# Hybrid decoder trunk: a fourth buffer for the gated levels, a new pace of the projections that fill the attention steps, and another order of three parts of a step

## The reference, cut to what matters

```python
z = h @ w_in[l]
(g_q, g_k, g_v, g_lr, g_r, d_q, d_k, d_v, i_q, i_k, i_w, c_u) = jnp.split(z, split_at, axis=-1)
# gated linear attention, 4 heads: decays are exp of differences of a running sum b of log_a
o_gla = gla_chunked(g_q, g_k, g_v, log_a)
# sparse attention, 6 heads: 128 of the causal keys of each query, chosen by an indexer
o_dsa = dsa_attention(dq, dk, d_v, i_q, i_k, i_w * (IDX_HEADS ** -0.5), rel_bias, topk)
# causal depthwise convolution with 31 taps over 256 channels
o_conv = conformer_conv(c_u, conv_w[l], conv_b[l], conv_ln_g[l], conv_ln_b[l])
mix = jnp.concatenate([o_gla, o_dsa, o_conv], axis=-1)
x = x + mix @ w_out[l]
```

## Time and profile before

| | us |
|---|---|
| median of 3 executions | 1520.78 (1519.08 to 1529.86) |
| the profiled execution, its own time | 1523.78 |
| its span in the profile | 1521.9 |
| PE busy, of the span | 1428.2 (94%) |
| DVE busy | 1159.8 (76%) |
| ACT busy | 908.5 (60%) |
| POOL busy | 552.1 (36%) |

### The profile page before, as it was taken

How to read it: one execution, slowest core, us unless ns; L and a number is a source line. 1 busy time by engine, 2 the same in 40 slices (tenths; PEclk the granted TensorE clock), 3 DMA queues, 4 the chain that set the end, 5 groups by cost and what they waited for, 6 DMA issues and landing times.

```text
span 1521.9 us, 20214 instructions
## 1 busy us (share of the span) xinstructions
PE 1428.2 (94%) x6710; PEld 1036.4 (68%) x6710; DVE 1159.8 (76%) x1658; ACT 908.5 (60%) x1346; POOL 552.1 (36%) x240
## 2 busy tenths in 40 slices
PE   7999989999899999999799999999988999999996
PEld 4677455567577888877556864565766778887773
DVE  4697877433479999999758968773334899999997
ACT  5643445743547888788475533448335488887881
POOL 2332242060005666554542413311500066555544
PEclk9999999999989999999999999999989899999999
DMA  6332601312239999999651431105040499999995
GB/s 226 93 91 62 220 1 56 141 56 88 79 123 338 401 399 399 398 399 399 215 193 43 111 100 52 56 1 196 1 165 1 180 350 399 399 399 398 398 401 192
DMA packets 151483, 312.73 MB, mean 205 GB/s; under 512 B 33158, under 2 KB 46380, under 8 KB 151228
## 3 DMA queue, kind: packets, MB, share of 16 engines
q1 hardware_dynamic: 140300, 271.39, 49.3%
q0 software_dynamic: 6624, 24.12, 4.3%
q10 hardware_dynamic: 4496, 16.40, 2.7%
HBM read 287.76 MB, written 29.50 MB: 208 GB/s over the span
## 4 chain that ended last, share of the span: by engine, by line
PE 47%; DVE 24%; DMA 15%; ACT 7%; issue 6%; DVEq 1%; POOL 0%; SPq 0%; POOLq 0%; ACTq 0%
PE ps L708 13%; DMA arena<-in_w_down 12%; DVE rest_w_down L1425 8%; PE ps L726 6%; PE ps L1502 5%; DVE rest_w_up L1425 4%; PE ps L1524 3%; DVE rest_w_gate L1425 2%; ACT head_w_down L1420 2%; PE ps L815 2%; DVE xg_rest L1438 2%; PE ps L1618 2%; PE ps L729 1%; PE ps L788 1%; PE ps L1637 1%
## 5 line engine op out<-in xcount | busy, mean ns | idle before, releaser
L2088 POOL TENSOR_TENSOR rest_w_down<-arena,head_w_down 128x2048 fp32r<-128x2048 f32 x30 | 191.2, 6372 | 191.5 <-ACT head_w_down L1420 191.5
L1425 DVE TENSOR_TENSOR rest_w_down<-arena,head_w_down 128x2048 fp32r<-128x2048 f32 x30 | 152.1, 5069 | 13.3 <-ACT head_w_down L1420 13.2
L1425 DVE TENSOR_TENSOR rest_w_gate<-arena,head_w_gate 128x2048 fp32r<-128x2048 f32 x64 | 145.9, 2280 | 0.1
L1425 DVE TENSOR_TENSOR rest_w_up<-arena,head_w_up 128x2048 fp32r<-128x2048 f32 x64 | 143.5, 2281 | 0.1
L1420 ACT ACTIVATE head_w_down<-arena 128x2048 fp32r<-128x2048 f32 x60 | 115.2, 1926 | 39.3 <-DMA arena<-in_w_down 39.0
L1420 ACT ACTIVATE head_w_gate<-arena 128x2048 fp32r<-128x2048 f32 x60 | 114.8, 1919 | 37.0 <-DMA arena<-in_w_gate 37.0
L1420 ACT ACTIVATE head_w_up<-arena 128x2048 fp32r<-128x2048 f32 x64 | 122.0, 1940 | 10.5 <-DMA arena<-in_w_up 10.5
L1409 PE MATMUL ps<-head_w_gate,xg_head 128*128 128x512 f32 x256 | 104.0, 406 | 3.7 <-DVE xg_rest L1438 2.7
L1399 PE MATMUL ps<-head_w_down,he_head 128*128 128x512 f32 x240 | 99.7, 415 | 6.5 <-DVE rest_w_down L1425 3.8
L726 PE MATMUL ps<-hT,arena 128*128 128x512 f32 x224 | 105.1, 608 | 0.7 <-ACT mixg L936 0.7
L1411 PE MATMUL ps<-head_w_gate,xg_rest 128*128 128x512 f32 x256 | 100.1, 391 | 0.0
(11 more groups left out here) (373 smaller groups left out, 3516.1 us busy)
## 6 DMA issues: line engine op xcount, KB each, us to landing
arena<-in_w_gate SPq DMA_DIRECT2D x64, 1024.0 KB, 10.1
arena<-in_w_up SPq DMA_DIRECT2D x64, 1024.0 KB, 10.7
arena<-in_w_down SPq DMA_DIRECT2D x64, 1024.0 KB, 10.4
arena<-in_w_in SPq DMA_DIRECT2D x10, 1536.0 KB, 6.7
yrows<-yb ACTq DMA_DIRECT2D x30, 512.0 KB, 6.2
arena<-in_w_in SPq DMA_DIRECT2D x4, 2048.0 KB, 8.5
x<-in_x SPq DMA_DIRECT2D x8, 512.0 KB, 13.8
arena<-in_w_in SPq DMA_DIRECT2D x16, 256.0 KB, 4.7
```

The lines of the kernel that those rows point to most:

```text
L1425: nc.vector.tensor_tensor(wl[q][:, c, :], raw[q][:, c, :], wh[q][:, c, :].bitcast(F32), ALU.subtract).then_inc(s_split[q], 1)
L2088: nc.gpsimd.tensor_tensor(wl[2][:, c, :], raw[2][:, c, :], wh[2][:, c, :].bitcast(F32), ALU.subtract)\
```

## The change

- A fourth level buffer: the tile `rs`, which holds the roots of the gated outputs later in the layer, is added to `lev`. Levels use `lev[v % 4]`; the diagonals move to `lev[3]`. `differences(v)` waits from v = 3 on, for the diagonals (v = 3) or for the products of level v-4.
- The planner gets three ranges: steps 0 to 3 for ca and cg, 4 to 8 for gq and gk, 9 to 21 for the rest. gk's last piece falls in step 8 in place of 9. By the planner's arithmetic the pieces of steps 4 to 17 become 6, 7, 6, 6, 7, 7, 6, 6, 6, 5, 6, 4, 5, 4 (before: 6, 6, 6, 5, 6, 7, 6, 7, 6, 5, 6, 5, 4, 5), and the third update falls in step 16 in place of 17.
- `LEV0` loses its "- 1", so it stays at step 8. `FACTORED` becomes 9 (from 10), the step of `states` 17 (from 18).
- `FIRST_TAP` becomes 5 (from 4). The taps of steps 4 to 21 become 0, 6, 6, 6, 5, 2, 0, 1, 1, 1, 2, 3, 3, 3, 6, 6, 5, 6 (before: 2, 6, 6, 6, 4, 4, 2, 0, 0, 0, 1, 2, 3, 6, 3, 6, 5, 6).
- In PE's even steps the values come straight behind the turn, then the first piece of projection, then the logits, then the second piece.

```diff
-            lev = [view(mixg[:, :, :].rearrange("p h s -> p (h s)"), 1024 * i, 2, S) for i in range(2)] + [sq[:, :, :]]
+            lev = [view(mixg[:, :, :].rearrange("p h s -> p (h s)"), 1024 * i, 2, S) for i in range(2)] + [sq[:, :, :], rs[:, :, :]]
...
-            GATED, LAST_FILLED, FIRST_O = 4, 22, 19
+            GATES, GATED, LAST_FILLED, FIRST_O = 4, 9, 22, 19
...
-            first, then = range(GATED), range(GATED, LAST_FILLED)
-            paces = [filler(("ca", "cg"), first) / len(first), filler(("gq", "gk", "gv", "kt", "gr", "upd", "o"), then) / len(then)]
+            phases = ((("ca", "cg"), range(GATES)), (("gq", "gk"), range(GATES, GATED)),
+                      (("gv", "kt", "gr", "upd", "o"), range(GATED, LAST_FILLED)))
+            paces = [filler(names, steps) / len(steps) for names, steps in phases]
...
-                pace += paces[n >= GATED]
+                pace += paces[(n >= GATES) + (n >= GATED)]
...
-            LEV0 = step_of(done("gk") - 1) - 1
+            LEV0 = step_of(done("gk") - 1)
...
-            FIRST_TAP, LAST_TAP, MEAN = step_of(done("cg") - 1) + 1, 21, 22
+            FIRST_TAP, LAST_TAP, MEAN = step_of(done("cg") - 1) + 2, 21, 22
...
                     turn(n)
+                    if n % 2 == 0 and n:
+                        values(n - 2)
+                    for job, c in work_of[n][:1]:
+                        work(job, c)
                     if n % 2 == 0 and n + 2 < NS:
                         logits(n + 2)
                         logits(n + 3)
-                    if n % 2 == 0 and n:
-                        values(n - 2)
-                    for job, c in work_of[n][:2]:
+                    for job, c in work_of[n][1:2]:
                         work(job, c)
...
-                    if v >= 2:
-                        dve.wait_ge(sN["lev_mm"], v - 1)
+                    if v >= len(lev) - 1:
+                        dve.wait_ge(sN["lev_mm"], v - len(lev) + 2)
...
-                        do(nc.gpsimd.tensor_tensor(lev[2], gq, gk, ALU.mult), "lev_k")
+                        do(nc.gpsimd.tensor_tensor(lev[3], gq, gk, ALU.mult), "lev_k")
```

More of the change, by code:

```diff
@@ L771, in diagonals @@
                         for i in range(2):
-                            last = nc.tensor.matmul(ps[2][:, 4 * c + 2 * i:4 * c + 2 * i + 2], lev[2][:, i, P * c:P * c + P], gated,
+                            last = nc.tensor.matmul(ps[2][:, 4 * c + 2 * i:4 * c + 2 * i + 2], lev[3][:, i, P * c:P * c + P], gated,
                                                     start=True, stop=True)
@@ L785, in level_products @@
                             o = ps[LEV_BANK[h % 2]][:, at:at + 64].rearrange("p (n w) -> p n w", w=HALVES[v])
-                            k = lev[v % 3][r, h // 2, P * c:P * c + P]
+                            k = lev[v % len(lev)][r, h // 2, P * c:P * c + P]
                             q = k.rearrange("p (n w) -> p n w", w=2 * HALVES[v])[:, :, HALVES[v]:]
@@ L1073, in level_decays @@
                     act.wait_ge(sN["lev_d"], v + 1)
-                    d = halves(lev[v % 3], half)
+                    d = halves(lev[v % len(lev)], half)
                     nc.scalar.activation(d[:, :, half:], d[:, :, half:], ACT.Exp)
@@ L1231, in differences @@
                         dve.wait_ge(sN["proj_out"], done("cg"))
-                    if v >= 2:
-                        dve.wait_ge(sN["lev_mm"], v - 1)
+                    if v >= len(lev) - 1:
+                        dve.wait_ge(sN["lev_mm"], v - len(lev) + 2)
                     bv = halves(b, half)
-                    do(nc.vector.tensor_tensor(halves(lev[v % 3], half), bv, bv[:, :, half - 1:half].to_broadcast([P, 2 * S // (2 * half), 2 * half]),
+                    do(nc.vector.tensor_tensor(halves(lev[v % len(lev)], half), bv, bv[:, :, half - 1:half].to_broadcast([P, 2 * S // (2 * half), 2 * half]),
                                                ALU.subtract), "lev_d")
@@ L1241, in level_queries @@
                     dve.wait_ge(sN["lev_e"], v + 1)
-                    d = halves(lev[v % 3], half)[:, :, half:]
+                    d = halves(lev[v % len(lev)], half)[:, :, half:]
                     do(nc.vector.tensor_tensor(d, halves(gq, half)[:, :, half:], d, ALU.mult), "lev_q")
@@ L1356, in level_keys @@
                     gp.wait_ge(sN["lev_e"], v + 1)
-                    d = halves(lev[v % 3], half)[:, :, :half]
+                    d = halves(lev[v % len(lev)], half)[:, :, :half]
                     do(nc.gpsimd.tensor_tensor(d, halves(gk, half)[:, :, :half], d, ALU.mult), "lev_k")
```

## The result

| | median of 20 executions, us |
|---|---|
| before | 1523.42 (1518.83 to 1531.75) |
| changed | 1529.12 (1522.61 to 1537.57) |

The ratio is 1.0037, with a 95% interval of 1.0019 to 1.0055: slower by some 5.7 us, where 5.9 us less had been forecast, and 7 us above the upper end of the forecast's range. The profiled execution took 1525.32 us.

What follows compares the result with a forecast made beforehand. PE was taken as the bound, only its idle time and clock losses winnable: 17.4 us gain less 10.0 put back less 1.5 for the clock gave 5.9, so 1514.9 us. Its own range was 1511 to 1519, widened to 1507 to 1522.

Steps and rivals of the forecast that it cites:

- 6.4 us a layer: PE's waits before the turns, level products and turned keys: the most that could be won there in each layer.
- The 1.0 us before the first level products: Step 11, before L788: PE would newly wait about 1.0 us for merge(0), bounds 0 and 2.
- the three slow stretches: Clock drops behind PE's waits at step 11 and the turned keys: 1.55 us each, 4.6 us together to be won.
- the turned keys: PE's wait before L740: of 2.1 us a layer 0.3 would be left, bounds 0 and 2.1.
- the queue behind gk: Steps 9 and 10: DVE idles about 5.2 us, so PE waits 3.1 us at step 10's turn, bounds 2.5 and 3.8.
- Costed at nothing: Later first taps, earlier zeroing of states and values ahead of logits were priced at zero; uncovered logits would cost 1.3 us.
- In steps 15 to 21 ... 0.6 us, an estimate, bounds 0 and 1.5: Loss per layer as the third update waits for ACT's copy and DVE has less slack against PE.
- what would make it fail as a whole: PE meeting a wait in none of the listed places, above all for DVE in steps 17 to 21.
- B: Rival: every DVE operation queued behind gk meets Pool, PE waits 6.8 us at step 10's turn; 1523.9 us, chance 0.1.
- C: Rival: waits only move, 3.8 us at step 10's turn, turned keys wait as before; 1523 us, chance 0.13.
- -12.8 + 10.0 = -2.8: PE's waits in both layers: 6.4 us a layer won, 5.0 a layer put back.
- -4.6 + 1.5 = -3.1: Clock losses in both layers: three slow stretches won, 4.6 us, and 1.5 put back for one of two layers.

Runs made afterwards that it cites:

- e3: The kernel before with the fourth buffer and its later waits alone: steps 119.3 + 120.7 us, ratio 0.9906.
- e7: The kernel before with the fourth buffer and the new order in PE's even steps: steps 123.1 + 124.8 us, ratio 0.9977.
- e1: The changed kernel with the old order, logits back ahead of the values and the first piece: steps 125.5 + 128.3 us, ratio 1.0004.
- e5: The changed kernel with the old order and the decays in step 10; buffer, new pace and later taps stay: steps 122.7 + 122.5 us, ratio 0.9945.
- e2: The changed kernel with the decays to the end back in step 10: steps 124.9 + 126.4 us, ratio 0.9978.
- e8: The kernel before with the fourth buffer and values ahead of the logits, both pieces behind both: steps 122.0 + 122.0 us, ratio 0.9931.
- e4: The kernel before with the new order in PE's even steps alone: steps 129.8 + 132.2 us, ratio 1.0068.
- e11: The kernel of e5 with the states back in step 18: steps 119.0 + 118.8 us, ratio 0.9880.
- e6: The kernel before with the fourth buffer and the taps from step 5 on: steps 118.7 + 119.0 us, ratio 0.9916.
- e9: The kernel of e5 with PE's diagonals ahead of the last four pieces of step 10: steps 120.6 + 120.6 us, ratio 0.9908.
- e10: The kernel of e6 with the diagonals ahead of the last four pieces of step 10: steps 118.4 + 118.4 us, ratio 0.9899.
- e12: The kernel of e11 with the diagonals ahead of the last four pieces of step 10: steps 116.9 + 116.9 us, median 1504.64 us, ratio 0.9878.

## Why the prediction was wrong

**Right: what the buffer gives in PE's waits.** The mechanism and the places are those of e3. The 6.4 us a layer less 1.0 that it leaves behind make 10.8 for both; e3 measured 10.5 us of waits less. The 1.0 us before the first level products was 1.0 in the changed kernel too (L789 for L1262).

**Wrong: the three slow stretches, 4.6 us.** e3's trace has lost as much to the clock as that of the kernel before, 5.1 us: the two at step 11 stayed, the one behind the turned keys went, and another stands at step 17. The changed kernel's has lost 6.8 us, against a forecast of 3.1 less than before. Two of the three stood at step 11, where there was little to win: with one the step lasts 9.07 us (e3, layer 0), without one 9.35 (e7, layer 0), since PE then waits 1.0 + 1.2 us in it, for DVE's merge and for the next turn, in place of 0.4. Only the one behind the turned keys was paid for (step 15 of layer 1, 8.32 us for 6.75), and in its place came those at step 19.

**Right: the queue behind gk.** Predicted: DVE idle 5.2 us, the inverse of step 10 at 194.0, PE's wait 3.1 (2.5 to 3.8). Measured 4.76, 194.24 and 2.60. (The sum for gk's arrival, 186.19 + 0.57 + 0.09, makes 186.85 and not 186.95; DVE started at 187.76.) Only the split was off: I had the decays lengthened to 3.3 us by Pool, but DVE came 0.04 us ahead of it, and the two taps were lengthened, from 1.53 to 3.53. The Trainium skill (SBUF — State Buffer, "SBUF: two separate sides") says that whoever starts first holds the shared port pair for its whole instruction, and the trace agrees: Pool's product, started 0.04 us behind DVE's decays, ended 2.23 us after them (2.21 after L1243 in the kernel before), and the tap that started meanwhile took 2.74 us, 0.75 alone, and ended 0.55 us behind the product. Unlike the forecast, the clock stayed at 1.00 right behind the 2.60 us in both layers; it fell at step 11 (0.72 from 205 to 210 us).

The step cost more than its waits. e1 to e5 puts the decays in step 9 at 8.5 us of the steps, where 2 x 2.6 = 5.2 us are PE's wait at the turn of step 10. The rest is not DVE's lost time coming out later: PE's wait at step 19 is 2.99 us in both layers of both kernels. In the traces it is the clock. Step 10 of layer 1 in e1, then in e5:

```profile
943.57:952.56 8.99, 8.99 (x42) 5.67 (x43) 6.08 (x8) 3.57 (x9) 5.30 (x5) 0.81 0.00 0
938.57:945.99 7.42, 7.42 (x43) 4.94 (x42) 4.69 (x6) 4.94 (x9) 6.65 (x6) 1.00 0.00 1
```

The mean granted clock over all executions points the same way: it is 0.972 in the changed kernel and in e1, with the decays in step 9, and 0.975 and 0.976 in e2 and e5. 0.003 of 1525 us is some 4.6 us, and the ratios put the decays at 9 us in either pair.

**Wrong: "Costed at nothing", the values ahead of the logits.** The prediction said that DVE reads the logits in the next step, "which covers it", and named the price if it does not, 1.3 us in each even step where DVE leads. The cover was never checked against a row. The trace of before had one: at step 21 DVE already stood 0.41 us before the logits of step 22.

```profile
269.50 0.69 DVE L1209 CUSTOM_DVE_ANT_0 scratch<-ps,scratch 128x512 f32<-128x512 f32 x1 [0.41 <-PE ps L839]
```

DVE leads PE by a whole step there, so the step between is no cover: the logits had no slack, and DVE's wait grew by all of the delay (e8, e7). With the buffer the order costs 7.8 us of the steps (e7): 5.7 at steps 19 and 21 and 3.1 in PE's own products, a cost that the prediction didn't have at all, less 1.0 at steps 10 and 11. The delay was 1.4 us at step 6 and 2.1 at step 20, not 1.3. The other prices, 11.0 alone (e4 to before), 6.0 in e5 (to e2) and 1.7 in the changed kernel (to e1), differ by 5.1, 3.4 and -3.4 us lost to the clock. Behind the early states the part at step 19 falls away, since PE waits 2.9 us there already; what the order adds in the changed kernel is 1.3 us at step 21 and some 1 us of products a layer.

**Wrong: "In steps 15 to 21 ... 0.6 us, an estimate, bounds 0 and 1.5".** This term had no row under it. It measured 2.9 + 1.4 us of PE's waits a layer. The 2.9 at step 19 come from the earlier states, which with the slow stretch behind that wait cost 3.7 us a layer of the steps (e5 to e11); the 1.4 at step 21 come from the order, as they are not in e1 and e5. In layer 1 the clock was at its lower level, 0.50, for the 5 us behind the wait. The states were looked at for PE (the update that waits for ACT's copy) and for Pool, not for DVE, on which they wait 4.34 us with three taps and the inverse of step 18 queued behind. The earlier trace rows left that wait out. The kernel before has it too, in DVE's timeline at its step 18, with six taps done in the step ahead of it:

```profile
243.99 5.04 DVE L1226 SCALAR_TENSOR_TENSOR mixr<-arena,cf,mixr 128x512 f32<-128x512 f32 x6
...
253.62 1.78 DVE L1277 SCALAR_TENSOR_TENSOR arena<-arena,ebl 128x192 f32<-128x192 f32 x4 [3.70 <-ACT arena L948]
```

**Why the last two were missed.** "PE is the bound" was read from busy shares, 124 us against DVE's 101. But the chain of inverse, scaling and turn passes through DVE in every step, and PE, once ahead, waits for it. DVE's lead in steps 17 to 21 was the margin that two parts of the change spent: the wait for the states, now without the six taps ahead of it, and the logits. The prediction named this place as what would make it fail as a whole, without a price. Of the rivals none was right: B and C had the sign, by other mechanisms; the turned keys, on which C turns, wait for nothing in the changed kernel.

**The sum again, by kind** (the steps of both layers in the two traces; the forecast's terms in brackets, in us). PE's waits went from 17.7 to 18.9, +1.1 (-12.8 + 10.0 = -2.8); what is lost to the clock from 5.1 to 6.8, +1.7 (-4.6 + 1.5 = -3.1); PE's own products, which are what is left, +1.6 (0). Together +4.5. The 0.2 us of steps 2 and 4 lie ahead of the measure and add 0.8, so 5.3 of the 5.7 us are found.

By part, adding one after the other (e3, e6, e5, e1, changed): buffer -11.0, taps -2.3, pace with its early states +7.6 (of which the states 7.5), decays in step 9 +8.5, order +1.7: together +4.5. What is lost to the clock moves in these five by 0, -3.4, +3.4, +5.1 and -3.4 us, so a single term is good to one or two slow stretches. The taps are such a term, and no more is shown of them.

**Open.** The median moved by 14 us for e3, while the steps won 11. The mean granted clock points to the difference: over all executions it was 0.976 in e3 and 0.971 in the kernel before in the same rounds, some 7 us, while the two traces have 0.974 both; where in the kernel that lies, no run shows. And why one and the same wait brings a slow stretch in one layer and none in the other stays open.

## What to carry to other kernels

Where one engine is filled up with movable work, its busy share hides who sets the pace: read for each queue how far it leads at the steps where they meet, and follow every wait that a change adds to the leading engine to the next place where that engine waits anyway. Up to there it is spent from the lead, and behind it no more: the 4.8 us for gk cost PE 2.6 at the next turn and nothing at step 19, since DVE waits 4.3 us for the third update in between.

"The next step covers it" needs the row that shows the reader a step behind, and a wait of 0.4 us on that very pair is the sign that it isn't. Look also at what stands next to what in a queue: 0.2 us in each even step came from parting two pieces. And where two traces of unlike kernels are compared by a stretch, take out first what each has lost to the clock.

Put an operation that waits for a long chain behind the work that doesn't depend on it: moving the states one step back, behind six taps, was worth 3.7 us a layer, 1.7 of it the clock.

## What the runs showed of the hardware that had not been expected

A wait of PE of 2.60 us at step 10 left the granted clock at 1.00 in both layers of the changed kernel; in e1 the same wait was followed by 0.50 at once in layer 1 and not in layer 0. One of 2.91 us at step 19 left it at 1.00 in layer 0 of the changed kernel, while in layer 1 the same wait was followed by 5 us at 0.50, and the products of L727 then took 3.78 us for four in place of 1.98, as PE's timeline of the changed kernel has it a few us before and behind:

```profile
1012.04 1.98 PE L727 MATMUL ps<-hT,arena 128*128 128x512 f32 x4
1020.43 3.78 PE L727 MATMUL ps<-hT,arena 128*128 128x512 f32 x4 [2.91 <-ACT mixg L939]
```

In the kernel before 2.1 us had been enough in one layer and not in the other. Five kernels (changed, e1, e2, e5, e9) have a wait of 2.9 to 3.0 us at step 19, and in nine of these ten layers the clock is at 0.50 for a part of step 19 or 20; with 0.9 us or less there (e3, e6, e10, e11, e12) it is at 1.00 in all ten. At step 17 a wait of 0.8 us was enough in four layers (one each of e3 and e7, both of e8) and not in the ten others that have it. The length of a wait alone does not tell whether the clock falls; of one kernel's two equal layers one can lose 1.7 to 3.4 us more. And a slow stretch is paid only where PE would not wait otherwise: at step 17 it made 9.2 us of 7.5, at step 11 0.3 us or nothing (9.05 us with it and 8.75 without in the two layers of e11; 9.07 with it in e3, 9.35 without in e7).

Parting two pieces of one projection by another kind of product cost PE 0.2 us without a wait: 6.76 us for 6.57 with the same products (e4, step 6).

An operation that stands still for another engine is recorded as a long one: a tap of 128x512 took 2.74 us beside Pool's product of 128x1024 and 0.75 alone. Which of the two engines stands still is a matter of 0.04 us: Pool started first in the kernel before (197.10 and 197.14 us) and DVE's difference took 2.53 us; DVE started first here (187.76 and 187.79) and Pool's product took 3.41, 2.2 of them behind DVE's end.
